# The first gate tile's products with h, placed between the last steps of two attention stages

## The reference

```
ys = stack([y_a, y_d, y_f, y_s])                       # each (L, 256)
proj = einsum('blnc,ncd->blnd', ys, w_branch)          # (L, 4, 1024)
gates = sigmoid(g)                                     # g = h @ w_in[gate columns], (L, 4, 1024)
y = sum(gates * proj, axis=2) @ w_o
```

## Time and profile before

| | |
|---|---|
| the profiled execution | 1835.78 us, its span 1834.0 us |
| runs | 1838.7, 1833.24, 1838.27 us |
| mean clock granted to TensorE | 0.983 of full speed |
| TensorE matmuls busy | 1742.1 us, 95% of the span |
| VectorE, ScalarE, GpSimd busy | 888.7, 592.0 and 647.1 us |
| memory traffic | 135.58 MB, 74 GB/s in the mean |

### The profile page before, as it was taken

The page is one execution under the profiler, slowest core; times in us unless marked ns, Lnnn a source line. Parts: engine busy times, 40 slices in busy tenths (PEclk is TensorE's granted clock), DMA queues, the critical chain, the costliest instruction groups (busy, mean ns, idle before and its releaser), DMA issues.

```text
span 1834.0 us, 22463 instructions
## 1 busy us (share of the span) xinstructions
PE 1742.1 (95%) x8340; PEld 1454.7 (79%) x8340; DVE 888.7 (48%) x1576; ACT 592.0 (32%) x965; POOL 647.1 (35%) x363
## 2 busy tenths in 40 slices
PE   2999999999999999899999979999999999999996
PEld 2887878877888888797887768888888888888885
DVE  5615646469999999275754252221122122022116
ACT  2434234472232222364334473212122112211213
POOL 0521221004356565401884444224214322321424
PEclk9999999998999999999999989999999999999998
DMA  8121131011111111503764212112102111111202
GB/s 302 57 82 45 59 96 39 9 50 32 54 43 54 46 43 63 166 1 137 284 203 161 81 35 69 35 46 65 49 23 69 57 34 46 57 34 46 69 23 92
DMA packets 36292, 135.58 MB, mean 74 GB/s; under 512 B 4496, under 2 KB 4496, under 8 KB 36240
## 3 DMA queue, kind: packets, MB, share of 16 engines
q1 hardware_dynamic: 34000, 127.55, 20.6%
q0 software_dynamic: 2240, 7.34, 1.9%
HBM read 118.62 MB, written 9.96 MB: 70 GB/s over the span
## 4 chain that ended last, share of the span: by engine, by line
PE 89%; DVE 5%; ACT 3%; DMA 2%; issue 1%; POOL 1%; SPq 0%; DVEq 0%; ACTq 0%
PE ps L484 26%; PE ps L486 26%; PE ps L485 26%; PE ps L673 4%; PE ps L652 2%; PE ps L578 1%; PE ps L579 1%; DMA region_b<-in_w_ada 1%; DVE region_a L1569 1%; DVE h_t L1535 1%; ACT y_t L873 1%; ACT region_d L1030 0%; PE ps L684 0%; PE ps L504 0%; DVE region_a L1583 0%
## 5 line engine op out<-in xcount | busy, mean ns | idle before, releaser
L484 PE MATMUL ps<-h_t,w_t 128*128 128x512 f32 x1632 | 640.6, 392 | 6.1 <-POOL w_t L1107 2.4
L485 PE MATMUL ps<-h_t,w_t 128*128 128x512 f32 x1632 | 637.6, 391 | 0.0
L486 PE MATMUL ps<-h_t,w_t 128*128 128x512 f32 x1632 | 637.3, 391 | 0.0
L484 PEld LDWEIGHTS ps<-h_t,w_t 128*128 128x128 f32 x1632 | 308.0, 189 | 73.6 <-issue 4.0
L486 PEld LDWEIGHTS ps<-h_t,w_t 128*128 128x128 f32 x1632 | 307.8, 189 | 64.5
L485 PEld LDWEIGHTS ps<-h_t,w_t 128*128 128x128 f32 x1632 | 308.1, 189 | 64.1 <-issue 0.5
L1107 POOL TENSOR_TENSOR w_t<-raw,w_t 128x1280 fp32r<-128x1280 f32 (+1 forms) x67 | 183.2, 2734 | 251.3 <-ACT w_t L833 161.1
L1578 DVE TENSOR_TENSOR region_d<-ps,region_d 128x512 f32<-128x512 f32 x44 | 30.4, 692 | 439.8 <-PE ps L486 439.8
L1583 DVE TENSOR_TENSOR region_a<-ps,region_a 128x512 f32<-128x512 f32 x176 | 121.1, 691 | 109.5 <-PE ps L486 109.5
L1344 DVE MAX8 top<-region_b 128x8 f32<-128x384 f32 (+5 forms) x192 | 157.9, 882 | 17.3 <-issue 16.7
L1347 DVE MATCH_REPLACE8 region_b<-top,region_b 128x384 f32<-128x384 f32 (+5 forms) x192 | 166.1, 876 | 0.0
(11 more groups left out here) (184 smaller groups left out, 2182.2 us busy)
## 6 DMA issues: line engine op xcount, KB each, us to landing
raw<-in_w_ffn SPq DMA_DIRECT2D x66, 512.0 KB, 3.5
region_b<-in_w_ada SPq DMA_DIRECT2D x48, 512.0 KB, 4.4
raw<-in_w_gates SPq DMA_DIRECT2D x32, 640.0 KB, 3.9
raw<-in_w_z SPq DMA_DIRECT2D x18, 512.0 KB, 3.3
raw<-in_w_o SPq DMA_DIRECT2D x16, 512.0 KB, 3.6
region_a<-in_x SPq DMA_DIRECT2D x8, 512.0 KB, 11.7
mix_dram<-region_a SPq DMA_DIRECT2D x8, 512.0 KB, 6.0
region_a<-mix_dram SPq DMA_DIRECT2D x8, 512.0 KB, 6.6
```

The lines of the kernel that those rows point to most:

```text
L484: pe.matmul(o, a_hi, m_hi, start=first, stop=False)
L485: pe.matmul(o, a_hi, m_lo, start=False, stop=False)
L486: return pe.matmul(o, a_lo, m_hi, start=False, stop=last)
```

## The change

`attention` takes the number T of a gate tile. In its last two units and behind its last `values`, a generator (`gate_beside`) issues the tile's 48 matmuls with h in groups of six (two k-tiles): one group behind `turn(u)` and one behind `values(u - 1)` of each of the two last units, one behind the last `values`, and three behind the last `turn_out`. They go to bank 4 (first half) and bank 5 (second half). `gate_first` then does only the 12 matmuls with y of that tile, `gate_tile` the next tile, and the loop the remaining six. ACT reads the first tile from bank 4 + half. This is done for T_AFS in the attention that ends with SWA and for T_GD in the DSA attention. SP, POOL and VectorE keep their programs.

```diff
--- before.py
+++ after.py
@@ -685,21 +685,50 @@
                                       y_tok[g % 2][:, c * P:(c + 1) * P], ident)
                 mm.then_inc(s_turned, 1)
 
-            def attention(u0, n):
+            def attention(u0, n, gate=None):
+
                 end = u0 + n
+                beside = gate_beside(gate)
                 logits(u0)
                 logits(u0 + 1)
                 for u in range(u0, end):
                     if u + 2 < end:
                         logits(u + 2)
                     turn(u)
+                    if u >= end - 2:
+                        next(beside)
                     if u - 2 >= u0:
                         turn_out(u - 2)
                     if u > u0:
                         values(u - 1)
+                    if u >= end - 2:
+                        next(beside)
                 turn_out(end - 2)
                 values(end - 1)
+                next(beside)
                 turn_out(end - 1)
+                for _ in beside:
+                    pass
+
+            def gate_beside(T):
+
+                if T is None:
+                    for _ in range(5):
+                        yield
+                    return
+                pe.wait_ge(s_w_lo, T + 1)
+                for half in range(2):
+                    for k in range(KT):
+                        c, w = slice(half * HALF, (half + 1) * HALF), slice(k * P, (k + 1) * P)
+                        product(ps[:, 4 + half, :], w_t[:, T % 2, 0, w], w_t[:, T % 2, 1, w], h_hi[:, k, c],
+                                h_lo[:, k, c], k == 0, k == KT - 1)
+                        if k % 2:
+                            yield
+
+            def gate_first(T, buf):
+
+                for half in range(2):
+                    tile_half(ps[:, 2 + half, :], T % 2, half, KT, BT, y_hi(buf), y_lo(buf)).then_inc(s_z, 1)
 
             z_group(T_FOX, 2)
             forget_sums(0)
@@ -721,34 +750,42 @@
             pe.wait_ge(s_moved[T_FOX + 3], 32)
             pe.wait_ge(s_lo_odd, 64)
             pe.wait_ge(s_lo_even, 32)
-            attention(U_FOX + 2 * TT, 2 * TT + TT)
+            attention(U_FOX + 2 * TT, 2 * TT + TT, T_AFS)
             pe.wait_ge(s_pt, U_DSA)
             pe.wait_ge(s_of, O_DSA)
 
-            def gate_pairs(T0, buf):
-
-                with pe.Fori(0, KT // 2) as i:
+            def gate_tile(T, buf, i=0):
+
+                pe.wait_ge(s_w_lo, i * 2 + (T + 1))
+                for half in range(2):
+                    pe.wait_ge(s_zf, i * 4 + (2 * T + half - 1))
+                    tile_half(ps[:, half, :], T % 2, half)
+                    tile_half(ps[:, 2 + half, :], T % 2, half, KT, BT, y_hi(buf), y_lo(buf)).then_inc(s_z, 1)
+
+            def gate_pairs(T0, buf, n=KT // 2):
+
+                with pe.Fori(0, n) as i:
                     for j in range(2):
-                        pe.wait_ge(s_w_lo, i * 2 + (T0 + j + 1))
-                        for half in range(2):
-                            pe.wait_ge(s_zf, i * 4 + (2 * (T0 + j) + half - 1))
-                            slot = (T0 + j) % 2
-                            tile_half(ps[:, half, :], slot, half)
-                            tile_half(ps[:, 2 + half, :], slot, half, KT, BT, y_hi(buf), y_lo(buf)) \
-                                .then_inc(s_z, 1)
+                        gate_tile(T0 + j, buf, i)
+
+            def gate_pairs_begun(T0, buf):
+
+                gate_first(T0, buf)
+                gate_tile(T0 + 1, buf)
+                gate_pairs(T0 + 2, buf, KT // 2 - 1)
 
             pe.wait_ge(s_ya, 1)
-            gate_pairs(T_AFS, 0)
+            gate_pairs_begun(T_AFS, 0)
             gate_pairs(T_AFS + KT, 1)
             pe.wait_ge(s_ys, 1)
             gate_pairs(T_AFS + 2 * KT, 0)
             z_group(T_DSA, T_GD - T_DSA)
             pe.wait_ge(s_moved[T_DSA], 32)
             pe.wait_ge(s_key_in, 64)
-            attention(U_DSA, HEADS * TT)
+            attention(U_DSA, HEADS * TT, T_GD)
             pe.wait_ge(s_pt, U_DSA + HEADS * TT)
             pe.wait_ge(s_of, O_DSA + TT)
-            gate_pairs(T_GD, 1)
+            gate_pairs_begun(T_GD, 1)
 
 
             pe.wait_ge(s_ada_used, 6 * KT)
@@ -983,25 +1020,36 @@
             act.wait_ge(s_ya_in, 16 * BT)
             act.activation(y_hi(0), ya_back[:, :, :], ACT.Copy).then_inc(s_ya_hi, 1)
 
-            def gate_pairs(T0, m0):
-
-                with act.Fori(0, KT // 2) as i:
+            def gate_tile(T, m, i=0, bank=0):
+
+                for half in range(2):
+                    act.wait_ge(s_z, i * 4 + (2 * T + half + 1))
+                    act.wait_ge(s_mix, i * 4 + (MIX0 + m + half))
+                    act.activation(sig, ps[:, bank + half, :], ACT.Sigmoid)
+                    act.activation(prj, ps[:, 2 + half, :], ACT.Copy).then_inc(s_zf, 1)
+
+            def gate_pairs(T0, m0, n=KT // 2):
+
+                with act.Fori(0, n) as i:
                     for j in range(2):
-                        T = T0 + j
-                        split_hi(T + 1, i, 2, GT)
-                        for half in range(2):
-                            act.wait_ge(s_z, i * 4 + (2 * T + half + 1))
-                            act.wait_ge(s_mix, i * 4 + (MIX0 + m0 + 2 * j + half))
-                            act.activation(sig, ps[:, half, :], ACT.Sigmoid)
-                            act.activation(prj, ps[:, 2 + half, :], ACT.Copy).then_inc(s_zf, 1)
-
-            gate_pairs(T_AFS, 0)
+                        split_hi(T0 + j + 1, i, 2, GT)
+                        gate_tile(T0 + j, m0 + 2 * j, i)
+
+            def gate_pairs_begun(T0, m0):
+
+                split_hi(T0 + 1, n=GT)
+                gate_tile(T0, m0, bank=4)
+                split_hi(T0 + 2, n=GT)
+                gate_tile(T0 + 1, m0 + 2)
+                gate_pairs(T0 + 2, m0 + 4, KT // 2 - 1)
+
+            gate_pairs_begun(T_AFS, 0)
             act.activation(y_hi(0), y_s, ACT.Copy).then_inc(s_ys_hi, 1)
             gate_pairs(T_AFS + KT, 2 * KT)
             gate_pairs(T_AFS + 2 * KT, 4 * KT)
             z_group(T_DSA, T_GD - T_DSA)
             attention(U_DSA, HEADS * TT)
-            gate_pairs(T_GD, 6 * KT)
+            gate_pairs_begun(T_GD, 6 * KT)
             for dt in range(KT):
                 act.wait_ge(s_mix, MIX0 + 6 * KT + 2 * (dt + 1))
                 act.activation(h_hi[:, dt], z[:, dt], ACT.Copy).then_inc(s_mix_hi, 1)
```

## The result

The kernel after took 1840.2 us in the median of 20 runs, the kernel before 1836.91; the ratio of their times is 1.0017 (95% interval 1.001 to 1.0024), that is 3.1 us slower (1.8 to 4.4). The forecast was 5.4 us slower (1842.5 us). One of the 20 runs after took 3092.19 us, in a slow state with a mean granted clock of 0.674, and is left out of the ratio. The two profiled executions lie 5.1 us apart in span (1834.0 and 1839.1 us).

The account below looks back on a forecast made before the run. TensorE's own work was taken as the bound, 89% of the span. End A winning 2.0 us and end B losing 7.4 made 5.4 us slower, from 1837.0 to a forecast of 1842.5 us, range 1837 to 1848.5.

Parts of the forecast that it names:

- end B: End of the sparse (DSA) attention into branch D's gates: predicted 7.4 us lost, bounds 6.0 and 9.5.
- VectorE's delay: At end A, POOL's long subtraction holds VectorE's addition for unit 38 until 419.85, so PE waits 3.2 us.
- end A: End of the window attention into the first gates: 3.5 us won, less 1.5 for the clock; 2.0, bounds -1.3 and 6.7.
- The clock in the gates: At end B, PE's idle time leaves the second tile at a low clock: 1.7 to 2.9 us lost, 2.6 taken.
- The 0.5 for a fall in the tail: At end B, the clock may fall at about 849, delaying `s_of` by up to 1.7 us; 0.5 taken.
- upper bound of 9.5: The most that end B was predicted to lose, 9.5 us, against 7.4 forecast.
- The table load: At end A, ScalarE's activation table load, hidden before, was predicted to be on the path for 1.4 us.
- bound of 6.7 us for end A without VectorE's delay: At end A, if VectorE is not held, PE doesn't wait and 6.7 us are won.
- Rival 1: Clock stays up, VectorE escapes: end A brings 5 to 6.7, end B costs 6.0 to 6.5; about 1837.5 us; chance 0.17.
- Rival 2: At end B the read-back doesn't hold the second tile, 6.1 us won there; about 1827 us; chance 0.05.
- Rival 3: Clock falls in both tails and stays low into both gate stages, net 10.8 us lost; about 1848 us; chance 0.13.
- Rival 4: The moved products don't run beside anything, as their weights come late; about 1838 us; chance 0.02.

Follow-up runs that it names:

- e3_b_behind: The changed kernel with all 48 products with h at end B behind the last turn_out instead of between the steps; ratio to the kernel before 0.9979.
- e4_b_split: The changed kernel with POOL splitting the second gate tile's weights at end B before it waits for the read-back; ratio to the kernel before 0.9993.
- e9_clock47: The changed kernel with 47 matmuls without use put into PE's wait at end B; ratio to the kernel before 1.0008.
- e2_end_b: Only end B of the change, with end A as in the kernel before; ratio to the kernel before 1.0029.
- e1_end_a: Only end A of the change, with end B as in the kernel before; ratio to the kernel before 0.9983.
- e6_clock: The changed kernel with 36 matmuls without use put into PE's wait at end B; ratio to the kernel before 1.0021.
- e5_a_moved: Only end A of the change, the group behind turn(39) moved behind values(39) and one more group there; ratio to the kernel before 0.9951.
- e7_both: The changed kernel with end A's moved order and, at end B, early split, read-back awaited in two parts, one load earlier; ratio to before 0.9933.

## Why the prediction was right

Direction and place were right at both ends, and the mechanism at end B and of VectorE's delay at end A; two terms at end A were wrong and cancel. The sum, 5.4 us, was above the measured interval of 1.8 to 4.4.

**What bounds it; end B.** The step that carried the forecast was that the path at end B is `s_of`, read-back, split, and not PE's first tile. It predicted the read-back 4.3 us later, the second tile 25.0 us behind turn(70) and ten microseconds of idle PE; measured were 4.33, 24.78 and 9.73. e3_b_behind and e4_b_split show both links of it: moving the products behind the last turn_out, or the split ahead of the wait, takes the loss away. The clock in the gates was put at 2.6 and cost 2.77 (e9_clock47). The 0.5 for a fall in the tail was too much in this execution: granted 1.00 there. In the place of 7.4 us stand 6.8 in the trace of the kernel after, 6.0 in that of e2_end_b, where the last copy came 97.96 us behind the second tile, so 1.8 and not 2.8 for the clock, and 5.3 (3.5 to 7.2) in e2_end_b's runs. The upper bound of 9.5 doesn't follow from the terms given: 4.3, 2.9 and 1.7 make 8.9.

**End A.** The sequence that makes VectorE late was predicted to within half a microsecond: POOL first by 0.7 us (0.43), an addition of 3.85 us (4.13), PE's wait of 3.2 (3.46). The 2.0 us of gain came out as 2.0, but that was luck: two errors cancel. The table load was not on the path. I had put 1.4 us for it, since in the loop before it came behind the wait for the matmuls (429.70). In the unrolled code of this kernel ScalarE loads the table as soon as it is free, as this row of the kernel after shows, 17 us ahead of its use:

```profile
416.97 1.28 ACT L1028 ACT_TABLE_LOAD   x1
```

The second tile then started right behind the 12 matmuls with y. Against that, the low clock from about 422 to 429 (PE's windows above) cost more than the 1.5 us that I took: from turn_out(38) to the end of the last group of products it was 11.2 us where my working at the full clock had 8.0, so 3.2. PE had come to turn_out(38) 0.4 us sooner than worked out, so that the group ended 26.1 us behind turn(38) in the place of 23.3, 2.8 more. How long the clock stays low differs from execution to execution: of the six kernels with this order, e1_end_a had it low for some 3 us and took 27.33 for end A, after and e4_b_split for some 7 us (28.93 and 28.28), e3_b_behind, e6_clock and e9_clock47 for some 10 us (29.62 to 29.72). The three kernels in which it doesn't fall took 21.84 to 21.87. This is also why one profile can't give the net: it says 4.8 us, the 20 runs 3.1. Where the remaining 1.7 us lie was not settled. Both ends can hold a part: e1_end_a's runs won 3.1 us, against a mean of 2.0 in those six profiles, and e2_end_b's lost 5.3, against 6.8 in the profile of the kernel after.

The bound of 6.7 us for end A without VectorE's delay was too low, e5_a_moved won 9.1: the table load again 1.4, and 1.0 in PE's steps (the last product with h ended 19.1 us behind turn(38), 20.1 in my working).

**The rivals.** Rival 1 (clock up, VectorE free) did not happen in this kernel, but is what e5_a_moved makes at end A. Rival 2 (the read-back doesn't hold the tile) fell with e4_b_split: its second tile started 9.8 us earlier as soon as POOL did not wait. Rival 3 had the clock falling in both tails; it fell at end A alone. Rival 4 fell: the products run where they were put.

The rule of the Trainium skill on the shared memory interfaces (GPSIMD Engine Reference, Specifications) agrees with the sizes of this one addition: 0.16 us by itself, 1.84, 2.15 and 4.13 us beside POOL's subtraction, ending with it each time. By the rule of the Trainium skill on transposes and the clock (TensorE: Matmul & The Clock Gate, PE-mode transpose) the products may keep the clock up. The tails of end B agree with what it would do here: with products among the steps the clock stayed at 1.00 (850 to 855 in the kernel after and in e2_end_b), without them it fell between 847 and 850 in before, e1_end_a and e3_b_behind. But the products also filled PE's gaps, and no run separates the two. At end A of the kernel after they did not keep it up: it fell at about 422, just behind PE's wait of 3.46 us.

## What to carry to other kernels

Work put into an idle engine's gaps can delay whatever that engine has to issue next, here by 4.3 us. Before placing it, look for what the step behind the gap releases, here a store's read-back in another queue; place it behind that step, not ahead of it. When a tile becomes ready sooner, everything that was scheduled under its old duration has to come sooner too: its split, the next load, the wait that guards another buffer. A small VectorE addition with two inputs in SBUF, which took 0.16 us ahead of a long GpSimd subtraction and up to 4.13 beside it, belongs ahead of it, and here PE's order decided which came first.

## What the runs showed of the hardware that I had not expected

- The activation table was loaded ahead of the wait where ScalarE's instructions were unrolled (416.97, 17 us ahead of its use), and behind it in the loop before (429.70, 0.5 us after the issue of the last matmul that it waited for).
- The clock fell behind idle times of PE of 2.97 us (e6_clock, granted 0.57 from 872 to 874) and 2.23 us (e7_both, 0.73 from 880 to 885), though PE had been busy without a gap for over 8 us ahead of each; behind 1.96 us it did not (e3_b_behind, 1.00 from 865 to 870). In the tail of the kernel before it fell at about 849 with no wait of PE above 0.7 us in the two microseconds before it. So no length of a gap follows from these runs.
- At end A the same order of PE's work took from 27.33 to 29.72 us in six executions, and the low clock's length was what differed; in the order in which the clock stays up three executions agree within 0.03 us.
